# GpSimd takes six weight remainders of the hybrid layers' projections, and six top-k rounds move from the latent attention into the projections

## The reference

```python
x = x + 0.5 * swiglu(rmsnorm(x, ffn1_norm), ffn1_gate, ffn1_up, ffn1_down)
z = rmsnorm(x, mix_norm) @ w_in                    # 15 named pieces of z
y_a = dsa_mixer(aq, ak, av, iq, ik, iw, ...)       # attention over 128 selected keys per query
y_b = gla_mixer(bq, bk, bv, bg, br, ...)           # gated linear attention in 8 chunks
y_c = conv_mixer(cu, ...)                          # 31 tap convolution
y_d = mla_mixer(dcq, dckv, dkpe, ...)              # latent attention, 4 heads
x = x + concat(y_a, y_b, y_c, y_d) @ w_out
x = x + 0.5 * swiglu(rmsnorm(x, ffn2_norm), ffn2_gate, ffn2_up, ffn2_down)
```

```python
s = relu(einsum('bthd,bsd->bths', iqb, ik) * idx_scale)
score = where(causal, einsum('bths,bth->bts', s, wb), -inf)
_, sel = top_k(score, 128)
```

## Time and profile before

| | |
|---|---|
| median of 3 runs | 3483.84 us (3483.67 to 3484.84) |
| the profiled execution | 3482.52 us, its span 3480.7 us |
| PE busy | 3359.6 us, 97% |
| DVE busy | 1595.7 us, 46% |
| ACT busy | 1170.0 us, 34% |
| POOL busy | 411.5 us, 12% |
| PE's share of the chain that ended last | 90%; DVE 6%, ACT 2% |

### The profile page before, as it was taken

How to read it: one execution, slowest core, us unless ns; L and a number is a source line. 1 busy time by engine, 2 the same in 40 slices (tenths; PEclk the granted TensorE clock), 3 DMA queues, 4 the chain that set the end, 5 groups by cost and what they waited for, 6 DMA issues and landing times.

```text
span 3480.7 us, 39701 instructions
## 1 busy us (share of the span) xinstructions
PE 3359.6 (97%) x14384; PEld 2578.8 (74%) x14384; DVE 1595.7 (46%) x2295; ACT 1170.0 (34%) x1726; POOL 411.5 (12%) x285
## 2 busy tenths in 40 slices
PE   7999999999999999999899999999999999899998
PEld 5888775778887788876677888565678886668886
DVE  3332489643323433288834331944343327643322
ACT  4332345432323332245533321214333214543322
POOL 1110002111100110000211100400111003111100
PEclk9999999999999999999999999999999999999999
DMA  4333231033333333332023333440223332223332
GB/s 138 93 94 97 85 79 50 3 89 96 91 96 91 90 96 92 95 79 75 1 64 88 96 92 95 99 76 31 65 86 96 93 94 85 61 79 90 96 94 76
DMA packets 420124, 286.04 MB, mean 82 GB/s; under 512 B 57416, under 2 KB 395180, under 8 KB 419884
## 3 DMA queue, kind: packets, MB, share of 16 engines
q1 hardware_dynamic: 419200, 283.62, 28.5%
q10 hardware_dynamic: 828, 1.13, 0.1%
HBM read 280.24 MB, written 4.47 MB: 82 GB/s over the span
## 4 chain that ended last, share of the span: by engine, by line
PE 90%; DVE 6%; ACT 2%; issue 2%; POOL 0%; DMA 0%; DVEq 0%; ACTq 0%; SPq 0%; POOLq 0%
PE bank L856 26%; PE bank L857 26%; PE bank L858 25%; PE bank L851 1%; PE bank L1147 1%; PE bank L1146 1%; PE bank L1165 1%; PE bank L1261 1%; PE bank L1267 1%; PE bank L1384 1%; DVE small L2257 1%; PE bank L996 0%; PE bank L998 0%; PE bank L997 0%; PE bank L1348 0%
## 5 line engine op out<-in xcount | busy, mean ns | idle before, releaser
L858 PE MATMUL bank<-xn_lo,w_hi 128*128 128x512 f32 x2800 | 1097.5, 392 | 0.0
L856 PE MATMUL bank<-xn_hi,w_hi 128*128 128x512 f32 x2496 | 1000.2, 401 | 42.8 <-DVE xn_lo L1973 20.1
L1984 DVE TENSOR_TENSOR w_lo<-wring,w_hi 128x1024 fp32r<-128x1024 f32 x478 | 594.5, 1245 | 926.0 <-ACT w_hi L1511 925.1
L857 PE MATMUL bank<-xn_hi,w_lo 128*128 128x512 f32 x2496 | 989.3, 396 | 0.0
L1511 ACT ACTIVATE w_hi<-wring 128x1024 fp32r<-128x1024 f32 x490 | 517.6, 1059 | 1194.7 <-DMA wring<-in_ffn_down 358.5
L858 PEld LDWEIGHTS bank<-xn_lo,w_hi 128*128 128x128 f32 x2800 | 528.7, 189 | 132.5
L856 PEld LDWEIGHTS bank<-xn_hi,w_hi 128*128 128x128 f32 x2496 | 470.0, 188 | 165.0 <-issue 49.4
L857 PEld LDWEIGHTS bank<-xn_hi,w_lo 128*128 128x128 f32 x2496 | 470.8, 189 | 104.6 <-issue 2.6
L857 PE MATMUL bank<-h_hi,w_lo 128*128 (+1 forms) x1056 | 420.4, 398 | 0.0
L856 PE MATMUL bank<-h_hi,w_hi 128*128 (+1 forms) x1056 | 415.8, 394 | 0.0
L858 PE MATMUL bank<-h_lo,w_hi 128*128 (+1 forms) x1056 | 415.2, 393 | 0.0
(11 more groups left out here) (382 smaller groups left out, 2913.7 us busy)
## 6 DMA issues: line engine op xcount, KB each, us to landing
wring<-in_ffn_gate SPq DMA_DIRECT2D x88, 512.0 KB, 3.8
wring<-in_ffn_up SPq DMA_DIRECT2D x88, 512.0 KB, 3.8
wring<-in_ffn_down SPq DMA_DIRECT2D x88, 512.0 KB, 3.5
wring<-in_ffn_w_gate SPq DMA_DIRECT2D x44, 512.0 KB, 3.8
wring<-in_ffn_w_up SPq DMA_DIRECT2D x44, 512.0 KB, 3.8
wring<-in_ffn_w_down SPq DMA_DIRECT2D x44, 512.0 KB, 3.5
wring<-in_w_in SPq DMA_DIRECT2D x34, 512.0 KB, 3.7
wring<-in_w_out SPq DMA_DIRECT2D x16, 512.0 KB, 3.6
```

What stands on the lines that cost most here:

```text
L856: nc.tensor.matmul(ps, w_hi[:, slot, t, 0:M], hi, start=start, stop=False)
L857: nc.tensor.matmul(ps, w_lo[:, slot, t, 0:M], hi, start=False, stop=False)
L858: return nc.tensor.matmul(ps, w_hi[:, slot, t, 0:M], lo, start=False, stop=stop)
L1984: nc.vector.tensor_tensor(w_lo[:, slot, :, :].rearrange("p k c -> p (k c)"), wunit[:, slot, :], w_hi[:, slot, :, :].rearrange("p k c -> p ...
```

## The change

`Z_ROUNDS` grows by one round in each of n = 17 to 22 (from 2 to 3 at n = 17 to 20, from 3 to 4 at n = 21, from 5 to 6 at n = 22): six rounds more. As the sequence is one, every later place gets other rounds: the mixers now hold rounds 27 to 41 instead of 21 to 35, the latent attention 42 to 47 (i = 2 to 7) instead of 36 to 47 (i = 2 to 13). The remainders of units 17 to 22 leave `dve_z` and go to `pool_z`, behind the two gate products, where GpSimd first waits until `u_lo` has counted the 17 that VectorE has done. In the attention VectorE waits at i = 15 until all remainders of the projections are counted.

```diff
 Z_IDX = [0] * 10 + [3] * 6 + [2] * 3
 Z_TAPS = [0] * 4 + [6] * 8 + [4] * 2 + [3] * 2 + [0] * 7
-Z_ROUNDS = [0] * 14 + [1] * 2 + [3, 2, 2, 2, 2, 3, 5]
+Z_POOL = 17
+Z_ROUNDS = [0] * 14 + [1] * 2 + [3, 3, 3, 3, 3, 4, 6]
...
             for n in range(2, NZU):
-                dve_units(dve, st, n, n + 1)
+                if n < Z_POOL:
+                    dve_units(dve, st, n, n + 1)
                 dve_conv(dve, nc_, nc_ + Z_TAPS[n])
...
                 if 15 <= i < 15 + SLOTS:
+                    if i == 15:
+                        dve.e.wait_ge(u_lo.h, st.units)
                     dve_units(dve, st, i - 15, i - 14)
...
-        def pool_z(pool):
+        def pool_z(pool, st):
             for ct in range(2):
...
+            pool.e.wait_ge(u_lo.h, st.units + Z_POOL)
+            pool_units(pool, st, Z_POOL, NZU)
...
-                pool_z(pool)
+                pool_z(pool, STAGES["in", l])
```

## The result

| | median us (range, runs) | ratio to before, 95% interval |
|---|---|---|
| before | 3484.34 (3483.67 to 3485.78, 4) | |
| after | 3513.48 (3511.49 to 3515.07, 4) | 1.0082, 1.0070 to 1.0094 |

The forecast was slower, 3497, in a range of 3484 to 3503. The direction was right; the time lies 10 us above the range. The change costs 29 us where 13.6 were forecast. The profiled execution took 3514.66 us (span 3512.9, mean granted clock 0.980; before 0.987).

The account below looks back on a forecast made before the run. TensorE was taken as the bound, VectorE counting only where TensorE waits for it. 8.3 + 1.9 - 0.8 - 2.6 = 6.8 us a layer, 13.6 for two, on 3482.52 gave 3496.1; median 1.3 higher, said 3497, range 3484 to 3503.

Parts of the forecast that it names:

- Rounds added, remainders removed: Projections: six more rounds cost VectorE 7.5 us, five of six remainders taken away give 5.65, so it ends 1.85 us later.
- the collision: Projections: VectorE's short instructions stand until GpSimd's remainder ends, 8.0 us a layer, bounds 0 and 14.1.
- Walk: Following VectorE's order through the projections beside GpSimd's six remainders: four collide, 8.0 us; VectorE ends 9.85 us later.
- The 8.9 that stands beside it: Projections: the same collisions estimated by the skill's port rule, each costing the rest of GpSimd's instruction, 8.9 us.
- What is late next: Entry to the mixers: TensorE not held in the projections, L2197 8.3 us later, TensorE stands 9.8 us, half clock adds 1.9.
- bounds 0 and 2: Limits in us a layer on the 1.9 us for half clock behind TensorE's 9.8 us stand from L1085.
- Mixers, gain 0.8: Mixers: rounds at i = 4, 5 and 6 become 256 wide instead of 384, gaining 0.8 us a layer.
- Latent attention, 2.6: Steps i = 8 to 13 lose their rounds, winning 2.6 us a layer, ends 0.5 and 3.4.
- The first: Rival: GpSimd's remainders fall on rounds or beside waits, -3.1 us a layer, 3478; chance 12%.
- The second: Rival: collision as forecast, attention gives back 3.4 and the clock costs nothing, 4.1 us a layer, 3492; chance 20%.
- The third: Rival: VectorE's lateness reaches TensorE in the projections at the sixth norm, 3509 with the collision's bound of 14.1; chance 8%.
- the slack of 1.57 us: Start of the mixers: VectorE's wait for ScalarE before L2197, which absorbs 1.57 us of its lateness.

Follow-up runs that it names:

- e3: The kernel after, with GpSimd starting its remainders of units 19 to 22 only when VectorE has come to the rounds behind its short instructions; 3488.0 us.
- e5: The kernel after, with TensorE doing surplus products in two stands of each hybrid layer, 10 before L1086 and 5 before L1115; 3496.0 us.
- e7: e3 with TensorE doing 2 surplus products before L1086 and 5 before L1115; 3476.4 us.
- e10: The kernel after, with 5 surplus TensorE products before L1115 alone, the stand before L1086 left; 3501.7 us.
- e2: The kernel before, with only the remainders of units 17 to 22 moved to GpSimd and the rounds left where they were; 3490.9 us.
- e6: The kernel before, with TensorE doing 5 surplus products in its stand before L1114; 3482.6 us.
- e9: The kernel after, with 10 surplus TensorE products before L1086 alone, the stand before L1115 left; 3503.7 us.

## Why the prediction was wrong, point by point

- *Rounds added, remainders removed, and the collision:* right. Walk 8.0, measured 8.0 us, at the four places named (of the two tensor_scalars at unit 19 only the second stood). The 8.9 that stands beside it comes to 8.7 when its start times are taken with 2.35 us a remainder. End of the rounds 9.7 later, forecast 9.85. Shown by the trace, and by e3, which takes away the coincidence alone.
- *What is late next:* right (L2199 begins 7.8 us later than L2197 did, forecast 8.3; TensorE's stand 9.4, forecast 9.8; TensorE not held in the projections). Of the clock behind this stand I had forecast 1.9 us with "bounds 0 and 2". It was 3.3 (the shift at L1095 of 11.2 less e5's 7.9), above the bound: I had taken the 3.8 us of work at half clock before L1120 in the trace of before as its maximum. It lasted 6.7 us, and half of that is the 3.3. The trace of before could have told that 3.8 is no maximum: at 2230.7 us TensorE works for 10.2 us at half clock:

```profile
2230.70:2240.90 10.20, 10.20 (x32) 7.30 (x32) 10.10 (x4) 0.00 (x0) 10.12 (x4) 0.50 0.12 27
```

- *Mixers, gain 0.8:* not seen. The shift goes from 11.2 at L1095 to 11.9 at L1114; e5, at full clock, goes from 7.9 to 7.0, so the gain of 0.8 was there and the half clock at 600 to 604 us took it, and more.
- *L1114, L1120 and the first attention steps:* no term at all in the forecast. After has 2.7 us more up to the end of L1120 and 2.9 more in the first steps, e5 neither (-1.9 and +1.0). This is the step that failed: the forecast counted the clock only behind the new stand and let the old stand before L1114 cost what it had cost before. Behind it were 3.8 us of work at half clock before, and 15.5 after; half of the difference is 5.8, and the shift grew by 5.7 there (11.9 to 17.6).
- *Latent attention, 2.6:* right. By their row maxima the steps i = 8 to 13 win 2.8 us in the profiles of after, e5, e7 and e10 alike. By e2 and e6 some 1.2 of it is the dip of before, which these lack. The half clock behind L1115 reached into the attention up to i = 2 (634.8 us); from there the clock was 1.0, as forecast.
- *The sum:* the terms of VectorE and the attention made 4.9 a layer (8.3 - 0.8 - 2.6). e5 measures 5.9 by the medians and 3.7 by the shifts. The clock, in the sum with 1.9, is 8.8 by the medians and 11.3 by the shifts. So the term of the clock was too small by 7 to 9 us, twice, and the place where most of it fell was not in the sum. In the first layer of after's profile the 8.3 us between 6.8 and 15.1 are 1.0 up to L1095, 1.5 in the mixers, 5.7 behind L1115 and 0.1 in the rest of the attention.
- *The rivals.* The first ("the trade works as meant", 3478) needed the remainders beside rounds; e3 and e7 made them so, and it took the clock as well to get 3476. The second took the dip of the clock in the attention before for a cost to be won back, and it was one, 1.2 us a layer (e2, e6); it failed because the clock behind the stands cost what it took for nothing. The third didn't occur: the sixth norm had its margin.
- *The range.* Its upper end came from the collision's bounds and the third rival. No case gave the clock more than 2 us a layer, though both of before's dips were in the earlier trace rows.
- *A reading of the chain:* it leaves TensorE for ScalarE already at 564.8 us, and L2213 and a round on VectorE stand in it before L2197, which the forecast calls the first. No term hangs on it: the slack of 1.57 us ahead of L2213 is in the sum.

Left open: what makes the half clock behind a stand last 4 us of work or 16. The same instructions behind the same stand had both (e9, e2: first and second layer).

## What to carry to other kernels

Where TensorE was the bound here, a stand of it was charged with its length and with the work behind it at 1.2 GHz. That second part was larger than the first (8.3 us behind the stand of 4.6 in e9's first layer, 12.0 against e5's 3.7), and its price in one trace was a sample, not a bound. Before an engine's load is moved to GpSimd, walk down the other's order and put the new instruction beside work that it doesn't stop: here the whole kernel took 3488 us with four remainders beside rounds and 3513 with them beside short instructions. Whether a dip of the clock costs anything depends on which engine sets the pace in that stretch, and a change that relieves VectorE there makes the dip count. Busy time alone doesn't tell: the dip inside the attention cost 1.2 us with VectorE busy 13 of 14.

## What the runs showed of the hardware

- In one execution of e9 the same products behind the same stand have the full clock back after 16 us of work in the first layer and after 5 in the second, and TensorE is at work nearly all the while (13.77 of 14 us in the first). That it was slow is no artefact of the record: L1121's products take 421 ns each where L1120's have a median of 275. The Trainium skill, "TensorE: Matmul & The Clock Gate", "What's actually happening", says that the ramp varies from run to run and is below 1% of a typical span. Here what lay behind the two stands of each hybrid layer was 0.5% (17.5 of 3513), which agrees and was yet more than half of the change's effect.
- An fp32 product of 128x512 is two records of 0.43 us, 0.86 in all (8.75 us for ten), where I had put it at half.
- VectorE's maximum and its replacement ran beside GpSimd's remainders at 0.70 and 0.68 us, as alone (e3; the means of all are 0.69 and 0.68), while an instruction of 0.43 us stood for 2.53. The Trainium skill, "SBUF — State Buffer", "Who interferes with whom", has the port pair that the two share as an exclusive lock, held for a whole instruction; the trace agrees. GpSimd's remainder itself was 2.40 us alone and 2.62 to 2.68 in two of four collisions.
